# A 282 + 238 split of the 520 tokens, with the high and low part of the 238 in one product

## The reference

```python
def swiglu(h, w_gate, w_up, w_down):
    return (jax.nn.silu(h @ w_gate) * (h @ w_up)) @ w_down

def conv_module(h, hist, w_in, b_in, dw, dw_b, ln_g, ln_b, w_out, b_out):
    a = h @ w_in + b_in
    glu = a[..., :D_MODEL] * jax.nn.sigmoid(a[..., D_MODEL:])
    ...
    y = c @ w_out + b_out

for i in range(DEPTH):
    ...
    xp = xp + yp; xp = xp + swiglu(rmsnorm(xp, norm_ffn[i]), ...)
```

## Time and profile before

| | us |
|---|---|
| median of 3 runs | 2045.07 (2044.47 to 2051.78) |
| span of the profiled execution (its only time on the page) | 2049.0 |
| TensorE busy | 2003.5 (98%) |
| DVE busy | 1416.2 (69%) |
| ACT busy | 1060.2 (52%) |
| POOL busy | 255.0 (12%) |

### The profile page before, as it was taken

How to read it: one execution, slowest core, us unless ns; L and a number is a source line. 1 busy time by engine, 2 the same in 40 slices (tenths; PEclk the granted TensorE clock), 3 DMA queues, 4 the chain that set the end, 5 groups by cost and what they waited for, 6 DMA issues and landing times.

```text
span 2049.0 us, 41542 instructions
## 1 busy us (share of the span) xinstructions
PE 2003.5 (98%) x16576; PEld 1937.9 (95%) x16576; DVE 1416.2 (69%) x2412; ACT 1060.2 (52%) x1842; POOL 255.0 (12%) x253
## 2 busy tenths in 40 slices
PE   8999999999899999999999979999999999999999
PEld 7999999997599999999999859999999989999999
DVE  4994697468768946974466765895597269937952
ACT  5563465365355634653777753563365355624642
POOL 3000000169420000001111124000000120000001
PEclk8999999999999999999999999999999999999999
DMA  6233333244222333333532253233333313333332
GB/s 187 75 104 93 103 103 99 77 134 107 78 66 80 104 93 103 104 98 88 175 109 89 87 210 87 83 95 94 99 110 91 114 53 91 97 93 110 104 98 80
DMA packets 350021, 208.22 MB, mean 102 GB/s; under 512 B 9897, under 2 KB 340553, under 8 KB 349812
## 3 DMA queue, kind: packets, MB, share of 16 engines
q1 hardware_dynamic: 345988, 198.26, 33.4%
q0 software_dynamic: 3472, 6.96, 1.0%
q10 hardware_dynamic: 384, 0.55, 0.1%
HBM read 194.53 MB, written 8.60 MB: 99 GB/s over the span
## 4 chain that ended last, share of the span: by engine, by line
PE 82%; DVE 7%; POOL 4%; ACT 3%; issue 2%; DMA 1%; ACTq 0%; SPq 0%; POOLq 0%; DVEq 0%
PE acc L681 44%; PE pair L881 18%; PE acc L881 9%; PE bank L881 4%; POOL conv L2575 4%; PE pair L1083 1%; PE pair L762 1%; PE bank L1103 1%; DVE xn L1983 1%; DVE w_lo L1842 1%; PE pair L1058 1%; DMA hist_rows<-in_state_pool 1%; DVE w_lo L2019 1%; DVE block L2019 1%; DVE xt L2053 0%
## 5 line engine op out<-in xcount | busy, mean ns | idle before, releaser
L1316 ACT ACTIVATE w_hi<-raw 128x768 fp32r<-128x768 f32 (+1 forms) x220 | 199.3, 906 | 429.9 <-PE acc L681 426.7
L681 PE MATMUL acc<-h_hi,w_hi 128*128 128x260 f32 x1408 | 399.5, 284 | 0.0
L681 PE MATMUL acc<-h_lo,w_hi 128*128 128x260 f32 x1408 | 398.2, 283 | 0.0
L681 PE MATMUL acc<-h_hi,w_lo 128*128 128x260 f32 x1408 | 397.6, 282 | 0.0
L1842 DVE TENSOR_TENSOR w_lo<-raw,w_hi 128x768 fp32r<-128x768 f32 (+1 forms) x220 | 241.8, 1099 | 216.8 <-ACT w_hi L1316 211.4
L681 PE MATMUL acc<-xin_hi,w_hi 128*128 128x260 f32 x1152 | 331.8, 288 | 6.1 <-DVE w_lo L1842 4.9
L681 PE MATMUL acc<-xin_hi,w_lo 128*128 128x260 f32 x1152 | 325.5, 283 | 0.0
L681 PE MATMUL acc<-xin_lo,w_hi 128*128 128x260 f32 x1152 | 324.9, 282 | 0.0
L681 PEld LDWEIGHTS acc<-h_hi,w_hi 128*128 128x128 f32 x1408 | 265.2, 188 | 0.6
L681 PEld LDWEIGHTS acc<-h_hi,w_lo 128*128 128x128 f32 x1408 | 265.0, 188 | 0.0
L681 PEld LDWEIGHTS acc<-h_lo,w_hi 128*128 128x128 f32 x1408 | 264.8, 188 | 0.0
(11 more groups left out here) (441 smaller groups left out, 5301.3 us busy)
## 6 DMA issues: line engine op xcount, KB each, us to landing
raw<-in_ffn_w_gate SPq DMA_DIRECT2D x88, 512.0 KB, 4.0
raw<-in_ffn_w_up SPq DMA_DIRECT2D x88, 512.0 KB, 5.2
raw<-in_ffn_w_down SPq DMA_DIRECT2D x64, 384.0 KB, 3.6
raw<-in_ffn_w_down SPq DMA_DIRECT2D x64, 320.0 KB, 3.3
raw<-in_attn_w_qkv SPq DMA_DIRECT2D x24, 512.0 KB, 3.9
raw<-in_conv_w_in SPq DMA_DIRECT2D x16, 512.0 KB, 4.1
raw<-in_conv_w_out SPq DMA_DIRECT2D x8, 512.0 KB, 4.4
in_mix<-in_cache_k SPq DMA_DIRECT2D x8, 512.0 KB, 5.3
```

What stands on the lines that cost most here:

```text
L681: last = pe.matmul(acc[:, b, 0:HALF], w[:, w_tile * P:(w_tile + 1) * P], v[:, h * HALF:(h + 1) * HALF], start=start and t == 0, stop=stop ...
L1316: act.activation(w_hi[n.slot(2)][:, 0:cols], raw[:, q.slot(4), 0:cols], ACT.Copy).then_inc(split_hi, 1)
```

## The change

The tokens are divided 282 + 238 (FIRST, REST) instead of 260 + 260. The first part has three products of 282 columns as before. For the second part, the high and the low part of the input lie in one tensor (`xin`, `h_both`, `mix_both`), and one product of w_hi takes both, 2 x 238 = 476 columns, into one bank: columns 0 to 237 get w_hi x_hi, columns 238 to 475 get w_hi x_lo. A product w_lo x_hi of 238 columns is added to the first 238. So a step has five products. The second 238 columns must then be added to the first. The first part lies at the end of its bank, the second at the start of the next, so that the 520 results lie in one piece.

```diff
+BANK = 512
+FIRST = 282
+REST = T - FIRST
...
-            def half_products(m, h, w_tile, s, k_hi, k_lo, start, stop):
...
+            def first_part(m, w_tile, s, both, start, stop):
+
+                to = acc[:, 2 * m.slot(2), BANK - FIRST:BANK]
+                w = slice(w_tile * P, (w_tile + 1) * P)
+                pe.matmul(to, w_hi[s][:, w], both[:, 0, 0:FIRST], start=start, stop=False)
+                pe.matmul(to, w_hi[s][:, w], both[:, 1, 0:FIRST], start=False, stop=False)
+                return pe.matmul(to, w_lo[s][:, w], both[:, 0, 0:FIRST], start=False, stop=stop)
+
+            def second_part(m, w_tile, s, both, start, stop):
+
+                to = acc[:, 2 * m.slot(2) + 1, 0:2 * REST]
+                w = slice(w_tile * P, (w_tile + 1) * P)
+                pe.matmul(to.rearrange("p (x c) -> p x c", x=2), w_hi[s][:, w], both[:, :, FIRST:T], start=start, stop=False)
+                return pe.matmul(to[:, 0:REST], w_lo[s][:, w], both[:, 0, FIRST:T], start=False, stop=stop)
...
+            def take_extra(n, m):
+
+                act.wait_ge(units_done, n + 1)
+                if m:
+                    act.wait_ge(folded, folds_to(m - 1))
+                act.activation(spare[:], acc[:, 2 * (m % 2) + 1, REST:2 * REST], ACT.Copy).then_inc(extra_ok, 1)
...
+            def fold(m):
+
+                main = acc[:, 2 * (m % 2) + 1, 0:REST]
+                dve.wait_ge(extra_ok, copied_to(m))
+                dve.tensor_tensor(main, main, spare[:], ALU.add).then_inc(folded, 1)
+                dve.wait_ge(folded, folds_to(m))
+
+            def add_extra(m, to):
+
+                dve.tensor_tensor(to[:, FIRST:T], extra_of(m), to[:, FIRST:T], ALU.add).then_inc(folded, 1)
+                dve.wait_ge(folded, At(folds_to(m.start), m.step, m.i).v)
...
-                    dve.tensor_tensor(halves(gate_n[:]), accumulator(At(0)), halves(rstd[:]), ALU.mult).then_inc(evacuated, 1)
+                    fold(m0 + 2 * c)
+                    dve.tensor_tensor(gate_n[:], accumulator(At(0)), rstd[:], ALU.mult).then_inc(evacuated, 1)
...
-                        dve.tensor_tensor(halves(x[:, c, :]), accumulator(At(c)), halves(x[:, c, :]), ALU.add).then_inc(evacuated, 1)
+                        add_extra(At(m0 + DOWN_M[0] + c), x[:, c, :])
+                        dve.tensor_tensor(x[:, c, :], accumulator(At(c)), x[:, c, :], ALU.add).then_inc(evacuated, 1)
```

More of the change, by code:

```diff
@@ L101, in key_takes, with folds_to, copied_to @@
     return n // 3 + 1 if n % 3 == 2 else 2 * (n // 3) + n % 3 + 1
+JOINT = TILE["conv_out"]
+COPIED = [TILE[f"ffn{layer}"] + j for layer in range(4) for j in range(2 * PLAIN)]
+COPIED += [TILE["conv_in"] + j for j in range(2 * KT)] + [TILE["qkv"] + j for j in range(3 * HEADS)]
+def folds_to(m):
+    return m + 1 - (m >= JOINT)
+def copied_to(m):
+    return sum(1 for c in COPIED if c <= m)
 class At:
@@ L676, in _, with part_of, tile_products, unit @@
         def _(pe):
-            def half_products(m, h, w_tile, s, k_hi, k_lo, start, stop):
[L679 to L692, removed]
+            PARTS = (slice(0, FIRST), slice(FIRST, T))
+            def part_of(h):
+                return acc[:, 0, BANK - FIRST:BANK] if h == 0 else acc[:, 1, 0:REST]
+            def first_part(m, w_tile, s, both, start, stop):
[9 more added lines that the diff above has]
+                return pe.matmul(to[:, 0:REST], w_lo[s][:, w], both[:, 0, FIRST:T], start=False, stop=stop)
+            def tile_products(m, w_tile, s, both, start, stop):
+                first_part(m, w_tile, s, both, start, stop)
+                return second_part(m, w_tile, s, both, start, stop)
+            def unit(n, m, both, k0=0, k1=KT, kn_=KT, before=None):
                 pe.wait_ge(split_lo, (n + 1).v)
@@ L717, in before @@
                         means(r)
-                unit(n, m, xin_hi, xin_lo, before=before)
+                unit(n, m, xin, before=before)
                 if r in (1, 7):
@@ L869, in ffn @@
                 for j in range(1, 2 * PLAIN):
-                    unit(At(u + j), At(m0 + j), xin_hi, xin_lo)
+                    unit(At(u + j), At(m0 + j), xin)
                 def block(J, b):
@@ L962, in conv_mixer @@
                         else:
-                            unit(At(u + n), At(m0 + n), xin_hi, xin_lo)
+                            unit(At(u + n), At(m0 + n), xin)
                         if n == 12:
@@ L1630, in conv_mixer @@
                     n = At(u + 2 * i)
+                    take_extra(n.start, m0 + 2 * i)
                     split(n + 2)
@@ L2054, in ffn @@
                     dve.wait_ge(units_done, n.start + 2)
-                    dve.tensor_tensor(halves(up2[:]), accumulator(At(1)), halves(rstd[:]), ALU.mult).then_inc(evacuated, 1)
+                    fold(m0 + 2 * c + 1)
+                    dve.tensor_tensor(up2[:], accumulator(At(1)), rstd[:], ALU.mult).then_inc(evacuated, 1)
                     if c + 1 == PLAIN:
@@ L2208, in conv_mixer @@
                         dve.wait_ge(glu_ready, i)
-                    dve.tensor_tensor(halves(act_in[:, 0, :]), accumulator(At(0)), halves(rstd[:]), ALU.mult).then_inc(evacuated, 1)
+                    fold(m0 + 2 * i)
+                    dve.tensor_tensor(act_in[:, 0, :], accumulator(At(0)), rstd[:], ALU.mult).then_inc(evacuated, 1)
                     split(n + 2)
```

74 lines of the change are left out of this document (47 added, 27 removed).

## The result

2071.78 us median of four runs (2070.86 to 2076.50) against 2044.77 (2042.20 to 2051.78): ratio 1.013, 95% interval 1.0106 to 1.0154, some 27 us slower. I forecast 2022, and the range ended at 2061. The profiled executions differ by less, 2070.0 against 2049.0, because the last group of pool0's products begins at 42.13 us in the one and at 47.06 in the other; in the eleven traces of whole kernels it lies between 40.5 and 50.0, on the whole later the longer the granted clock was 0.50 ahead of it (not at all in the kernel after, 13.7 us in the kernel before), and not by what the kernel does.

A forecast was written before the change was run, and what follows sets the result against it. TensorE, busy 98%, was taken as the bound, with a 120 ns floor per product. -40.6 + 13.0 + 1.3 + 2.4 + 1.0 = -22.9 us: profiled span 2049.0 to 2026.1, median 2022, range 2007 to 2061.

The forecast's parts named there:

- TensorE's part: Product steps on TensorE: with a 120 ns floor, 681 against 720 ns a step; 1040 steps gain 40.6 us.
- reading (c): TensorE coming out of a wait: a weight load alone is some 107 ns, load and start together nearly 120.
- Reading (b): Eight float32r products at 1.2 GHz: 216 ns each, nothing added, so the cost is a maximum of two things.
- Reading (d): Against the load as bound: a transpose behind such a product also starts 0.12 us after it, despite its smaller load.
- Once per product: Rival, chance 0.20: 11.3 ns added to each product at 2.4 GHz, however wide; +6 us, 2051.
- Columns are the bound: Rival, chance 0.22: float32r streams some 2.25 columns a nanosecond, five products cost what six did; +15 us, 2060.
- The narrow product is slow: Rival, chance 0.05: a product of 238 columns costs 201 ns instead of 120; +93 us net, 2138.
- Folds nearly free: Rival inside the forecast, no chance of its own: floor holds, plain units cost 4 us instead of 13; 2013.
- Plain units and pairs behind: FFN plain units: copies and folds on DVE delay the pairs, 2 x 2.8 + 2 x 3.7 = 13.0 us lost.
- Pool stages and the end: Pool stages and the last tile of all: 1.0 us lost; more DVE work in the pool stages takes the gain back.
- Statistics: Means after a stage's last tile: DVE's extra add costs 0.6 us at four places, 2.4 us.
- Down, qkv, w_o, conv_out hidden: In these stages the later evacuation is hidden by a factor of four and costs nothing; qkv loop 7 us shorter.

The follow-up runs named there:

- e2: Changed kernel with its five products, but the extra 238 columns never copied nor added; 2051.79 us, ratio 1.002 to the kernel before.
- e1: Changed kernel with six products again, tokens still 282 + 238, nothing copied or folded; 2059.54 us, ratio 1.0059 to the kernel before.
- e3: Changed kernel with its folds, but the 476 columns issued as two products of 238; 2082.42 us, ratio 1.0166 to the kernel before.
- p1: Kernel before with the changed scheme in the 32 plain units only; 2060.00 us, ratio 1.0055.
- p2: Kernel before with the changed scheme in the two pool stages only; 2056.04 us, ratio 1.0037.
- p3: Kernel before with the changed scheme in the down projections, w_o and conv_out only; 2049.56 us, ratio 1.0018.

## Why the prediction was wrong

**The step that failed is TensorE's part**, the price of a product and with it of a step: "If 120 ns is a floor for a product and its load, the 282 just fit under it". It gave a step of 681 ns and -40.6 us; the step measured 722.6, and the five products without folds are some 4 us slower than the six (e2). There is a least time of a product with its load, but it is 111 to 112 ns, as the 224, 200 and 128 columns show, and 260 columns lie above it. The load of some 107 ns in reading (c) was near it; that load and start add up to the 120 was the error. What I took for the floor is columns/2.4 plus a toll that each of these float32r products pays at the full clock: in the kernel 12 ns with 260 columns, 14 with 282, 21 with 476, 11 with the 238 behind it. 6 x 12 is 72, 3 x 14 + 21 + 11 is 74: five products cost what six did. The experiments divide this further: 282 + 238 alone loses 9.4 ns a step (e1), since 282 has a higher toll than 260 and 238 runs into the least time three times; the join gives 8.3 back (e3 against after, in the kernel; the streams alone don't show it).

**Why I took it.** Reading (b), eight products at 1.2 GHz with nothing added, is right, and the 476 at half clock says it again. I took it to exclude a cost per product, "A cost that is always added, in time or in array cycles, would give 228 or 240", and chose the maximum. It excludes only one that is there at both levels; I had no row of another width at the full clock, so 120 could be split into a floor or a sum at will. Reading (d), a transpose also 0.12 us behind such a product, stood for a sum and I gave it too little.

**The rivals.** *Once per product* had the right form and the wrong size: 11.3 ns whatever the width, so a step of 709; it was 723, because the toll is larger with the new widths. *Columns are the bound* had nearly the right step (718 foreseen) and sign, with a mechanism that the 512 refutes (227 against 236); that the step came out right was luck, since a toll that grows with the width looks like a rate at 260, 282 and 476. Its time, 2060, was 12 us too low: it gained 2.6 us on the products where five products without folds lose some 4 (e2), and its folds were 5 short. *The narrow product is slow* fell: the 238 cost 110 to 113 ns. Its +93 us also counted 81 ns on all 1432 steps; on the 1040 that the other rivals use it would have been +61. *Folds nearly free* fell with p1.

**What the folds pay.** 17.7 us foreseen, some 22 measured.
- *Plain units and pairs behind*: 13.0 foreseen (3.7 twice, 2.8 twice); by the traces 14.1 (4.8 twice, 2.2 twice), by p1 11.3 with an interval of 7.6 to 14.7. The sum is right, the split is not quite. In layers 0 and 3 the 4.8 hold a second fall of the clock: the kernel after has it at 0.50 from 82.1 to 85.5 and from 1730.8 to 1734.2 us. Where it stayed at 1.00, in layer 3 of p1, the stretch is 3.7 us longer than before, just what I foresaw; the other 1.1 is the clock. The sign I gave, VectorE busy 95% or more in all layers, failed: 40.15 of 44.9 us in layer 0 and 38.33 of 43.3 in layer 1 are 89%. The prices were right: copy 0.35 us and fold 0.41 (medians of 72: 352 and 409 ns). The group of the fold, with the mean of one:

```profile
L1904 DVE TENSOR_TENSOR acc<-acc,spare 128x238 f32<-128x238 f32 x72 | 29.6, 410 | 50.8 <-ACT spare L1354 50.6
```

  The evacuation follows 0.45 us after the fold's start, within my 0.32 to 0.9.
- *Pool stages and the end*: 1.0 foreseen, 8.1 by the traces (3.3 and 4.9), 7.6 by p2. This is the second miss: I had counted "in the pool stages more work on DVE takes the gain back". But a tile there was 12 products, 1.4 us, beside some 1.2 us of evacuation for it, and VectorE also makes the low parts. Its 16 adds of 0.46 us stand in series with the products, and behind the longer waits the clock fell, 1.4 us more. In pool0 of p2 the granted clock stayed at 1.00, and its whole stretch up to the down projection lost 2.1 us.
- *Statistics*: 2.4 foreseen, at most half of it found: the down stretches of layers 0 and 1 with the means behind them are 0.3 us longer each, a third of that the steps' 1.2 ns; the same for w_o and conv_out is 0.2 and 0.4.
- *Down, qkv, w_o, conv_out hidden*: right for the down projections (p3) and for qkv: from the first product of its second unit to that of its last the loop takes 186.95 us before, 187.80 after, and 187.80 without the folds too (e2). It was foreseen 7 us shorter, which is the failed step again.
- *Conv_in*: +1.3 foreseen, -0.7 in the trace. Neither is settled: among kernels whose conv_in is as before, the stretch from its second unit to conv_out varies by 1.1 us (151.6 to 152.7).
- The table's 2.5 us for attention hold 1.5 in the decode part ahead of w_o, whose instructions did not change (65.5 and 67.0 us from the last product of qkv to the first of w_o). It is scatter: over the eleven traces this part takes 65.5 to 69.9 us, 66.5 in p1 and 69.0 in e1, which have no folds there. It is longest where the granted clock was longest at 0.50 beside it (6.8 us in the kernel before, 13.7 in e1).

The runs don't say what the toll is made of. It is not the adding up, the rows or the columns of weights; it goes with the type, and at 1.2 GHz it is not there. That the other engines add to it is not excluded. Streams of the step of before take 714 ns and the kernel 721, of six products of 282 and 238 720 and 731, of five of 264 and 256 707 and 716; only the change's five take 723 in both. The streams that had VectorE and ScalarE beside them had them in SBUF alone, not in PSUM, and without the kernel's transfers. This difference of 7 to 11 ns stays open.

## What to carry to other kernels

Before merging products, find out what one costs over its columns at several widths, because one width can't tell a floor from a sum: here 40 us hung on 12 ns read at 260 columns only. The width counts as much as the number of products: five products won 0.2% with 264 and 256 in the stages where the extra adds are free, and lost with 282 and 238. And ask, stage by stage, whether the engine that pays has slack; a wait of 2 us on TensorE can cost another 1.4 through its clock.

## What the runs showed of the hardware that I had not expected

- Float32r at 2.4 GHz pays 10 to 18 ns a product over its columns in a stream by itself (260: 10.4, 512: 13, 476: 15 to 18; 512 in two pieces 20), and narrow ones with their weight loads (224, 200, 128 columns) take 111 to 112 ns. Bfloat16 pays 2 to 3 (258 columns 110 ns, 502 212), and so does two-pass float32 over its two passes (500 columns 419 ns). The Trainium skill, "TensorE: Matmul & The Clock Gate", section Back-to-back issue gap, gives N/2.4 + 2.5 ns for the isolated gap and names no type there; the bfloat16 streams agree with it, and float32r is the exception here.
- Changing between bfloat16 and float32r at each product or two takes back what bfloat16 gains (717 ns for six against 714 all in float32r); in blocks of 16 and 32 it doesn't (119 and 111 ns).
- The starting column moves a 260-column stream by up to 5 ns (from 0: 118.9; from 1: 123.5; from 262: 122.5).
- Behind a wait of 2.3 us TensorE's granted clock was 0.50 for some 3.4 us, in pool0 and in pool1 of the kernel after; with 0.6 us of waiting in the same places before it stayed at 1.00. In pool0 of p2_pools and of e3_fold_no_join the same 2.3 us of waiting went by without it. So did a wait of 1.79 us in layer 3 of p1_plain, where in layer 0 the clock fell.
